# Router weights held in TensorE and tokens moved; routing of both token tiles in shared VectorE operations, experts chosen from the logits

## The reference

```
def moe_swiglu(h, router, w_gate, w_up, w_down):      # h: 256 x 1024, router: 1024 x 8
    probs = softmax(h @ router)
    vals, idx = top_k(probs, 2)
    gates = one_hot(idx) weighted with vals / sum(vals)   # 256 x 8
    for e in range(8):                                    # w_gate, w_up: 1024 x 2048, w_down: 2048 x 1024
        out += gates[:, e] * ((silu(h @ w_gate[e]) * (h @ w_up[e])) @ w_down[e])
```

## Time and profile before

| | before |
|---|---|
| median of 3 runs | 1415.55 us |
| lowest, highest | 1414.0, 1416.23 us |
| the profiled execution: its time | 1413.8 us |
| its span, first to last instruction | 1411.8 us |
| mean granted TensorE clock | 0.957 of 2.4 GHz |
| PE busy | 1323.1 us (94%) |
| DVE busy | 1049.4 us (74%) |
| ACT busy | 864.3 us (61%) |
| POOL busy | 38.8 us (3%) |
| mean DMA rate | 226 GB/s |

### The profile page before, as it was taken

How to read it: one execution, slowest core, us unless ns; L and a number is a source line. 1 busy time by engine, 2 the same in 40 slices (tenths; PEclk the granted TensorE clock), 3 DMA queues, 4 the chain that set the end, 5 groups by cost and what they waited for, 6 DMA issues and landing times.

```text
span 1411.8 us, 18829 instructions
## 1 busy us (share of the span) xinstructions
PE 1323.1 (94%) x6088; PEld 1080.8 (77%) x6088; DVE 1049.4 (74%) x1488; ACT 864.3 (61%) x1274; POOL 38.8 (3%) x54
## 2 busy tenths in 40 slices
PE   7999999997687899999999999999997985999998
PEld 5878888886566788888888888888886753888887
DVE  4576555565755799999999999999995846555554
ACT  4655444456533587878787887878784544454443
POOL 0000000000300000000000000000000211000000
PEclk9999999998887999999999999999998977999999
DMA  9645545554013397979898999889894400355540
GB/s 356 217 143 207 179 179 191 195 178 150 1 60 120 147 383 296 383 299 377 316 367 330 340 342 337 338 338 371 325 375 134 179 30 1 119 182 195 188 150 30
DMA packets 46121, 319.30 MB, mean 226 GB/s; under 512 B 5152, under 2 KB 6304, under 8 KB 7808
## 3 DMA queue, kind: packets, MB, share of 16 engines
q1 hardware_dynamic: 44288, 316.39, 59.7%
q10 hardware_dynamic: 1680, 2.10, 0.5%
q0 software_dynamic: 112, 0.26, 0.1%
HBM read 316.64 MB, written 2.10 MB: 226 GB/s over the span
## 4 chain that ended last, share of the span: by engine, by line
PE 84%; DVE 9%; issue 3%; ACT 3%; DMA 1%; DVEq 0%; POOL 0%; SPq 0%; ACTq 0%; POOLq 0%
PE bank L350 24%; PE bank L352 24%; PE bank L351 24%; PE bank L641 2%; PE bank L414 2%; DVE wl L1223 2%; DVE x L1637 1%; PE bank L744 1%; PE bank L386 1%; DMA fixed<-fixed_dram 1%; PE bank L660 1%; PE bank L661 1%; PE bank L765 1%; PE bank L581 0%; PE bank L803 0%
## 5 line engine op out<-in xcount | busy, mean ns | idle before, releaser
L1223 DVE TENSOR_TENSOR wl<-raw,wh 128x1024 fp32r<-128x1024 f32 x598 | 714.8, 1221 | 208.5 <-ACT wh L828 197.7
L828 ACT ACTIVATE wh<-raw 128x1024 fp32r<-128x1024 f32 x598 | 631.4, 1061 | 327.3 <-PE bank L352 320.6
L350 PE MATMUL bank<-wh,xth 128*128 128x512 f32 (+2 forms) x1170 | 464.1, 397 | 15.0 <-DVE wl L1223 4.7
L352 PE MATMUL bank<-wh,xtl 128*128 128x512 f32 (+2 forms) x1170 | 455.4, 389 | 0.0
L351 PE MATMUL bank<-wl,xth 128*128 128x512 f32 (+2 forms) x1170 | 455.1, 389 | 0.0
L350 PEld LDWEIGHTS bank<-wh,xth 128*128 128x128 f32 x1170 | 221.8, 190 | 61.2 <-issue 7.7
L352 PEld LDWEIGHTS bank<-wh,xtl 128*128 128x128 f32 x1170 | 221.4, 189 | 46.2
L351 PEld LDWEIGHTS bank<-wl,xth 128*128 128x128 f32 x1170 | 222.2, 190 | 42.3
L350 PE MATMUL bank<-wh,hth 128*128 128x512 f32 x456 | 178.5, 391 | 0.0
L352 PE MATMUL bank<-wh,htl 128*128 128x512 f32 x456 | 177.9, 390 | 0.0
L351 PE MATMUL bank<-wl,hth 128*128 128x512 f32 x456 | 177.4, 389 | 0.0
(11 more groups left out here) (281 smaller groups left out, 853.5 us busy)
## 6 DMA issues: line engine op xcount, KB each, us to landing
raw<-weights_dram SPq DMA_DIRECT2D x299, 1024.0 KB, 4.9
x<-x_dram SPq DMA_DIRECT2D x1, 1024.0 KB, 7.7
bias_scratch<-act ACTq DMA_DIRECT2D x1, 1024.0 KB, 15.7
wide<-bias_scratch ACTq DMA_DIRECT2D x8, 128.0 KB, 2.6
out_dram<-x SPq DMA_DIRECT2D x4, 256.0 KB, 2.1
fixed<-fixed_dram SPq DMA_DIRECT2D x1, 596.0 KB, 8.8
rows<-rows_dram POOLq DMA_DIRECT2D x1, 256.0 KB, 6.1
cols<-cols_dram SPq DMA_DIRECT2D x1, 73.0 KB, 8.5
```

Of the source, the lines that this page charges most:

```text
L350: mm(o, lh, wh[:, wi, sl], start=start, stop=False)
L352: return mm(o, ll, wh[:, wi, sl], start=False, stop=stop)
L828: A(wh[:, c % SPLIT, :], raw[:, (c // 2) % RAW, (c % 2) * UNIT:(c % 2 + 1) * UNIT], ACT.Copy).then_inc(hi_done, 1)
L1223: V.tensor_tensor(wl[:, c % SPLIT, :], raw[:, (c // 2) % RAW, (c % 2) * UNIT:(c % 2 + 1) * UNIT], f32(wh[:, c % SPLIT, :]), ALU.subtract). ...
```

## The change

It does five things.

1. The router's high and low weights become one tile `rw` of 16 columns for each block of 128 and are the stationary operand; `xth` and `xtl` (256 tokens) move past it. That gives 16 matmuls into 16 rows of logits parts by 256 tokens, half of them ahead of the second `turn_half`. ACT copies the 16x256 result to SBUF, and two small fp32 matmuls with a constant (`fold`, two stacked 8x8 identities) add the two parts and turn them back to tokens by experts. Low times low, left out before, is now in the sum.
2. DVE works on both token tiles in shared operations, and picks the experts from the logits; softmax comes no more.
3. The gates are made later, from the difference of the two largest logits with one small exponential on ACT; this DVE work stands between `sel` and `gathered`.
4. The five matmuls for places and counts become two for places ahead of the gather and two for counts (`bank[3]`) behind it; the copy to `queue` moves behind `gathered(0)`. Five fills of constants move ahead of the output projection, and ACT's part of `xn` moves behind the copy of the logits.
5. PE waits for the gathered blocks two at a time, ahead of each gate and up unit, in all 8 experts.

On PE:

```diff
             out_proj(U_WO, "ffn1")
+            def route(ks):
+                for k in ks:
+                    for x_part in (xth, xtl):
+                        last = mm(bank[0][0:2 * NE, 0:TOK], rw[:, k, :], x_part[:, k, :], start=(k == 0 and x_part is xth),
+                                  stop=(k == KD - 1 and x_part is xtl))
+                return last
+            pe.wait_ge(sem("rt_l"), 1)
+            pe.wait_ge(sem("norm_l"), KD * nth("ffn1") + 4)
+            route(range(0, 4))
             turn_half("ffn1", 1, 6)
-            pe.wait_ge(sem("norm_l"), KD * (nth("ffn1") + 1))
-            pe.wait_ge(sem("rt_l"), 1)
+            pe.wait_ge(sem("norm_l"), KD * nth("ffn1") + KD)
+            route(range(4, 8)).then_inc(sem("rt_L"), 1)
+            fold = fixed[0:2 * NE, FIXED["fold"]:FIXED["fold"] + NE]
+            pe.wait_ge(sem("rt_Lc"), 1)
             for t in range(NT):
-                for k in range(KD):
-                    h, l = xt(k, t)
-                    o = bank[t][:, 0:NE]
-                    mm(o, h, rth[:, k * NE:(k + 1) * NE], start=(k == 0), stop=False)
-                    mm(o, h, rtl[:, k * NE:(k + 1) * NE], start=False, stop=False)
-                    last = mm(o, l, rth[:, k * NE:(k + 1) * NE], start=False, stop=(k == KD - 1))
-                last.then_inc(sem("rt_S"), 1)
+                last = mm(bank[1][:, t * NE:(t + 1) * NE], ebuf[0:2 * NE, 0, t * P:(t + 1) * P], fold, start=True, stop=True)
+            last.then_inc(sem("rt_S"), 1)
-            pe.wait_ge(sem("chosen"), NT)
-            mm(bank[0][:, 0:NE], before, chosen[:, 0, 0:NE], start=True, stop=True)
-            mm(bank[0][:, 16:16 + NE], before, chosen[:, 1, 0:NE], start=True, stop=False)
-            mm(bank[0][:, 16:16 + NE], ones, chosen[:, 0, 0:NE], start=False, stop=True)
-            mm(bank[0][:, 32:32 + NE], ones, chosen[:, 0, 0:NE], start=True, stop=False)
-            mm(bank[0][:, 32:32 + NE], ones, chosen[:, 1, 0:NE], start=False, stop=True).then_inc(sem("places"), 1)
+            pe.wait_ge(sem("chosen"), 1)
+            mm(bank[2][:, 0:2 * NE].rearrange("p (t n) -> p t n", t=NT), before, chosen[:, :, 0:NE], start=True, stop=False)
+            mm(bank[2][:, NE:2 * NE], ones, chosen[:, 0, 0:NE], start=False, stop=True).then_inc(sem("places"), 1)
...
             gather("moe", sel, 1, CAP)
+            for t in range(NT):
+                last = mm(bank[3][:, 0:NE], ones, chosen[:, t, 0:NE], start=(t == 0), stop=(t == NT - 1))
+            last.then_inc(sem("counts"), 1)
             with pe.Fori(0, NE) as e:
-                pe.wait_ge(sem("moe_gl"), e * KD + KD)
                 ffn("ff", U_MOE, FFE // FG, 2, 3, FG, 2, e * 4, e, nt=1, done=DONE_FF1,
-                    early=lambda: scatter_and_turn(e), late=lambda: gather_next(e))
+                    early=lambda: scatter_and_turn(e), late=lambda: gather_next(e),
+                    rows_ready=lambda u: pe.wait_ge(sem("moe_gl"), e * KD + 2 * u + 2))
```

On ACT (the exponential before, L1064, goes), where `out_proj` has ended with the second half's `xth`:

```diff
             rs_ready("ffn1")
+            sc.wait_ge(sem("rt_L"), 1)
+            A(ebuf[0:2 * NE, 0, 0:TOK], bank[0][0:2 * NE, 0:TOK], ACT.Copy).then_inc(sem("rt_Lc"), 1)
             A(xn[:, 1, :], x[:, 1, :], ACT.Copy, scale=nrs[:, 1:2]).then_inc(sem("norm_xn"), 1)
+            sc.wait_ge(sem("rt_d"), 1)
+            A(small[:, 64:66], small[:, 62:64], ACT.Exp).then_inc(sem("rt_e"), 1)
```

On DVE; the loop over t that goes is L1551 to L1575, 17 operations for each tile:

```diff
+            link(V.memset(ones, 1.0))
+            link(V.memset(gates[:, :, :], 0.0))
+            link(V.memset(f32(selt[:, :]), 0.0))
+            link(V.memset(chosen[:, :, :], 0.0))
+            link(V.memset(place[:, :, :], 0.0))
             out_proj(U_WO, "ffn1")
             dv.wait_ge(sem("norm_rs"), nth("ffn1") + 1)
             V.tensor_scalar(xn[:, 0, :], x[:, 0, :], nrs[:, 0:1], None, ALU.mult)
-            link(V.memset(ones, 1.0))
-            link(V.memset(gates[:, :, :], 0.0))
-            link(V.memset(f32(selt[:, :]), 0.0))
...
+            dv.wait_ge(sem("rt_S"), 1)
+            link(V.tensor_tensor(lg, bank[1][:, 0:2 * NE].rearrange("p (t n) -> p t n", t=NT),
+                                 nrs[:, 0:NT, None].to_broadcast((P, NT, NE)), ALU.mult))
+            for t in range(NT):
+                r = V.max(top[:, t, :], lg[:, t, :])
+                link(r) if t else mark(r)
+            for t in range(NT):
+                r = V.max_index(topi[:, t, :], top[:, t, :], lg[:, t, :])
+                link(r) if t else mark(r)
+            link(V.tensor_copy(fi, topi[:, :, :]))
+            mark(V.tensor_tensor(first, io, fi[:, :, 0:1].to_broadcast((P, NT, NE)), ALU.is_equal))
+            link(V.tensor_tensor(second, io, fi[:, :, 1:2].to_broadcast((P, NT, NE)), ALU.is_equal))
+            V.tensor_tensor(chosen[:, :, 0:NE], first, second, ALU.add).then_inc(sem("chosen"), 1)
+            V.tensor_tensor(small[:, 62:64], top[:, :, 1], top[:, :, 0], ALU.subtract).then_inc(sem("rt_d"), 1)
             dv.wait_ge(sem("places"), 1)
-            link(V.tensor_copy(place[:, :, 0:NE], bank[0][:, 0:32].rearrange("p (t n) -> p t n", t=NT)[:, :, 0:NE]))
-            link(V.tensor_copy(queue[:, 0:NE], bank[0][:, 32:32 + NE]))
+            link(V.tensor_copy(place[:, :, 0:NE], bank[2][:, 0:2 * NE].rearrange("p (t n) -> p t n", t=NT)))
...
             ins.then_inc(sem("moe_sel"), 1)
+            dv.wait_ge(sem("rt_e"), 1)
+            link(V.tensor_scalar(small[:, 66:68], small[:, 64:66], 1.0, None, ALU.add))
+            link(V.reciprocal(small[:, 68:70], small[:, 66:68]))
+            link(V.tensor_tensor(small[:, 70:72], small[:, 64:66], small[:, 68:70], ALU.mult))
+            mark(V.tensor_tensor(first, first, small[:, 68:70, None].to_broadcast((P, NT, NE)), ALU.mult))
+            link(V.tensor_tensor(second, second, small[:, 70:72, None].to_broadcast((P, NT, NE)), ALU.mult))
+            link(V.tensor_tensor(gates[:, :, 1:NE + 1], first, second, ALU.add))
             gathered(0)
+            dv.wait_ge(sem("counts"), 1)
+            link(V.tensor_copy(queue[:, 0:NE], bank[3][:, 0:NE]))
```

More of the change, by code:

```diff
@@ L98 @@
 for _name, _n in (("ident", 128), ("mask", 384), ("ctab", 128), ("stab", 128), ("freq", 32), ("iota", 8),
-                  ("before", 128), ("slots", 128), ("every", 128)):
+                  ("before", 128), ("slots", 128), ("every", 128), ("fold", 8)):
     FIXED[_name] = _at
@@ L157, in build @@
         selt = sb("selt", [P, TOK], F32R)
-        rth = sb("rth", [P, KD * NE], F32R)
-        rtl = sb("rtl", [P, KD * NE], F32R)
+        rw = sb("rw", [P, KD, 2 * NE], F32R)
         small = sb("small", [P, 128])
@@ L465, in ffn @@
                 else:
-                    up(c0, i0)
+                    up(c0, i0, rows_ready)
                     early()
@@ L1057, in _ @@
                     A(xth[:, h, :], bank[4 + h % 2][:, 0:256], ACT.Copy).then_inc(sem("head_oh"), 1)
-            A(rth[:, :], cols[:, COLS["router"]:COLS["router"] + 64], ACT.Copy).then_inc(sem("rt_h"), 1)
+            A(rw[:, :, 0:NE], cols[:, COLS["router"]:COLS["router"] + 64].rearrange("p (k n) -> p k n", k=KD), ACT.Copy)\
+                .then_inc(sem("rt_h"), 1)
             out_proj(U_WO, "ffn1")
             rs_ready("ffn1")
+            sc.wait_ge(sem("rt_L"), 1)
+            A(ebuf[0:2 * NE, 0, 0:TOK], bank[0][0:2 * NE, 0:TOK], ACT.Copy).then_inc(sem("rt_Lc"), 1)
             A(xn[:, 1, :], x[:, 1, :], ACT.Copy, scale=nrs[:, 1:2]).then_inc(sem("norm_xn"), 1)
[L1062 to L1065, removed]
+            sc.wait_ge(sem("rt_d"), 1)
+            A(small[:, 64:66], small[:, 62:64], ACT.Exp).then_inc(sem("rt_e"), 1)
             def gathered(lot):
@@ L1541, in _ @@
             dv.wait_ge(sem("rt_h"), 1)
-            V.tensor_tensor(rtl[:, :], cols[:, COLS["router"]:COLS["router"] + 64], f32(rth[:, :]), ALU.subtract).then_inc(sem("rt_l"), 1)
+            V.tensor_tensor(rw[:, :, NE:2 * NE], cols[:, COLS["router"]:COLS["router"] + 64].rearrange("p (k n) -> p k n", k=KD),
+                            f32(rw[:, :, 0:NE]), ALU.subtract).then_inc(sem("rt_l"), 1)
+            link(V.memset(ones, 1.0))
[3 more added lines that the diff above has]
+            link(V.memset(place[:, :, :], 0.0))
             out_proj(U_WO, "ffn1")
@@ L1545, in _ @@
             V.tensor_scalar(xn[:, 0, :], x[:, 0, :], nrs[:, 0:1], None, ALU.mult)
-            link(V.memset(ones, 1.0))
-            link(V.memset(gates[:, :, :], 0.0))
-            link(V.memset(f32(selt[:, :]), 0.0))
-            for t in range(NT):
[L1551 to L1576, removed]
@@ L1577, in _ @@
-            link(V.memset(place[:, :, :], 0.0))
+            lg, top, fi, first, second = (small[:, 16 * n:16 * (n + 1)].rearrange("p (t n) -> p t n", t=NT) for n in (0, 1, 2, 5, 6))
+            io = fixed[:, None, FIXED["iota"]:FIXED["iota"] + 8].to_broadcast((P, NT, NE))
+            dv.wait_ge(sem("rt_S"), 1)
+            link(V.tensor_tensor(lg, bank[1][:, 0:2 * NE].rearrange("p (t n) -> p t n", t=NT),
```

(8 more changed lines are left out.)

## The result

The changed kernel took 1397.47 us in the median of 4 runs (1395.94 to 1398.22), the kernel before 1415.52 (1414.0 to 1416.23): ratio 0.9873, 95% interval 0.9855 to 0.989, 18.05 us less. Forecast were 1405.3 us, 10.2 us less, and 1402.0 to 1408.4 as range. The direction was right; the time lies 4.5 us outside the range.

What follows compares the result with a forecast made beforehand. PE was taken to bound the whole kernel (84% of the chain). The gather 10.75 us earlier, less 0.35 for its clock and 0.21 for the queue copy, gave 10.2 off 1415.55: 1405.3 us, range 1402.0 to 1408.4.

Steps and rivals of the forecast that it cites:

- first router half: Eight router matmuls in PE's pause after the output projection: cost 0, or 0.96 us without that cover.
- second router half: Eight router matmuls once `xtl` is ready, at half the clock with spacing 0.24: 2.1 us, bounds 1.2 and 3.6.
- routing on DVE: Shared DVE operations for both token tiles, after the fold: 1.9 us against 4.42, bounds 1.5 and 2.3.
- gather, later clock: First gather: the clock's rise comes 0.7 us later after its start, costing 0.35 us; bounds 1.9 either way.
- queue copy behind `gathered`: Copy to `queue` now on DVE's chain into the first expert: 0.21 us back.
- waits by twos: PE's waits for gathered blocks: gain 0, PE's first-turn pause about 2.4 us; rival that they pay: 1403.5 us, chance 0.05.
- net at both turns: From router to the first expert's turns: 10.75 less 0.35 less 0.21, 10.2 us gained.
- That bound: Lower bound for the router's second eight matmuls, at the full clock: 1.2 us.
- The gates are hidden as said: Six DVE operations between select and `gathered`, covered by the wait for the gather: cost 0, without cover 1.2 us.
- the rival's price: Pause at expert 0's first turn drops TensorE's clock: 1.6 us lost, 3 if longer; 1406.9 us, chance 0.25.
- the step to the total: What comes ahead of the expert loop moves the kernel's end one for one: 10.2 us off the median.
- the sign: Prediction is wrong if the span after expert 0's second turn differs in length from before.

Runs made afterwards that it cites:

- before_fillA: The kernel before with 29 matmuls that nothing reads, ahead of and in the last layer's first attention: 1411.1 us.
- after_serial: The changed kernel with gates, count matmuls and queue copy put back ahead of the gather: 1400.1 us in 2 runs.
- the three delayed ones: The changed kernel with 7, 14 or 21 linked fills on DVE ahead of select, a pure delay: 1404.77, 1403.52 and 1402.33 us.
- 7 fills: The changed kernel with 7 linked fills of 8 columns on DVE ahead of select: 1404.77 us.
- fillABM: Both kernels with 169 unread matmuls at the experts' end and around both last-layer attentions, none in the routing: before 1404.25 us, changed 1393.85.
- fillA: Both kernels with 29 unread matmuls ahead of and in the last layer's first attention: before 1411.1 us, changed 1400.26.
- before_router: The kernel before with the new router alone, DVE's routing still tile by tile: 1412.22 us, ratio 0.9982.
- after_again: The changed kernel, unchanged, run in a second session: 1402.37 us, ratio 0.9912.
- after_third: The changed kernel, unchanged, run in a third session: 1401.85 us, ratio 0.9912.

## Why the prediction was right and wrong

**Right: the stretch.** 11.1 us up to the loop's end against 10.2. By its terms, measured against forecast, in us:

| term | forecast | measured |
|---|---|---|
| first router half | 0 | 0 |
| second router half | 2.1 | 1.18 |
| copy of the logits | 0.44 | 0.43 |
| fold | 1.14 | 1.06 |
| routing on DVE | 1.9 | 1.62 |
| places | 1.14 | 1.13 |
| copy and select | 0.96 | 0.96 |
| sum, against 18.43 before | 7.68 | 6.38 |
| gather, later clock | 0.35 back | 0.83 back |
| queue copy behind `gathered` | 0.21 back | 0.41 back |
| waits by twos | 0 | not measured at the full clock |
| net at both turns | 10.2 | 10.8 |

That the net came out within 0.6 us is partly luck. The gather starts 12.05 us earlier and not 10.75, and two terms behind it, 0.7 us dearer together than forecast, take half of that back.

The biggest miss is the second router half. I took the low clock, since it had fallen by then in the kernel before; here it was still up (0.12 us spacing, 442.26 and 442.38). That bound was in the text, at 1.2. It was no chance of this one execution. With the first half in the pause ahead, the clock fell 6.6 to 7.1 us behind the start of the last projection matmul in all eleven traces without filling in the routing. In the kernel before it fell 3.6 us behind it in three traces, but 6.6 in the fourth (before_fillA), so even there the low clock wasn't sure. My doubled spacing of 0.24 was too dear as well: in before_fillA 14 matmuls with 256 columns moving, 128 stationary, took 3.00 us at the low clock, 0.21 each, which agrees with the estimate of 0.213 from the Trainium skill (TensorE: Matmul & The Clock Gate, section on the back-to-back issue gap). With 16 stationary columns no run shows the low spacing. On DVE an operation over 16 elements costs what one over 8 does (0.17 to 0.18 us), and the unlinked one of each pair costs 0.07 to 0.1. The gather's clock came back 5.5 us after its start and not 4.4. The last 0.3 us, between the second turn and the loop's end (10.8 to 11.1), lie in the loop; I did not follow them, and they are less than the 1.2 by which that stretch differs between traces of the changed kernel.

The gates are hidden as said: their last operation starts at 449.29, and DVE then waits 4.21 us for the gather's first half. Counts and queue copy would put the gather off by 1.05 us if they stood ahead of it (after_serial, expected 1.06), but with the clock back sooner the first turn by 0.12 only. What the waits by twos gained PE it gave back as forecast, in a pause of 3.01 us for `hbuf` (forecast 2.4). The pause kept the clock at 1.00 in the changed kernel's three traces and in five of its filled and changed variants, but it fell behind it in the three delayed ones, where the two turns lie 10.1 us apart and not 8.8: 1.3 us, the rival's price (1.6). The trace with 7 fills, pause and what follows:

```profile
465.00:469.00 4.00, 0.79 (x6) 0.52 (x5) 3.96 (x6) 0.38 (x1) 0.00 (x0) 1.00 0.26 59
469.00:473.00 4.00, 4.00 (x12) 3.10 (x11) 4.00 (x8) 1.44 (x2) 0.00 (x0) 0.57 0.95 367
```

Twelve matmuls in 4 us at 0.57. That rival is real: it came in 3 of 11 traces, its chance was put at 0.25. But it came in none of the three traces of the changed kernel itself, and in all three with a delay; whether the delay has a part in it isn't shown.

**Wrong: the step to the total.** The step that failed is the one that carries the net of the stretch to the end, 10.2 us off the median of before: it took what lies outside for equally long in both kernels, and gave it nothing in the range. It differs. The prediction had named the sign, a different length behind the second turn of expert 0: from there to the end of the span are 925.5 us before, and 919.0, 922.5 and 926.8 in the three traces of the changed kernel. The attention of the last layer took 28.9 to 37.0 us in the traces, with the same code but for the filling; the start of the routing lay between 436.7 and 439.6. In the kernel before, PE worked in that attention for most of 36 us and the clock stayed low for long; I read the clock there only for its pauses and not for what it would do when everything comes 11 us sooner. With the clock mostly held there in both, the change is worth 10.4 and 10.8 us (fillABM, fillA), which the forecast had. The result's 18 are these and a good clock: 6.8 of the 17.9 us between the profiles lie outside the stretch, and the mean clock is 0.968 in all four runs, of which one has a trace. The kernel before varies too: 1409.5 to 1419.4 in the 16 runs beside before_router, 1413.2 to 1417.0 in the 24 beside the delays and after_again.

The Trainium skill offers a cause (TensorE: Matmul & The Clock Gate, section on what's actually happening): the window in which the clock's monitor watches the engine is "free-running — it doesn't reset when your kernel starts". The runs agree that the course varies with nothing changed (the attention's 31.5, 33.1 and 37.0 us); that this is the reason no run here shows.

**Open.** Unfilled, the changed kernel gains 12 to 13 us in the later sessions and not 10.6, so it may meet a better clock a little more often than the kernel before; 14 runs against a spread of 9 us don't settle it. Nor is it shown why the first session's four runs were all fast, or whether the chip has a part in it: after_again ran on another chip than after_third, and that of the first session isn't on record.

## What to carry to other kernels

Put the rows of a change together as a chain and the stretch can be forecast, here to a microsecond with some luck among the terms; the total can't, where other stages run PE in bursts, as this attention does, since their clock can be another in each execution. Compare such kernels by landmarks in the trace, or in several sessions, or with PE's pauses filled in both (look in the trace whether the filling lies in the pause or behind it), and give the range the spread of those stages. Where an engine's second batch hides its partner's first, a faster engine alone brings that first batch onto the chain: the router gave 3.6 us of its 7.8 until DVE's work was shared too.

## What the runs showed of the hardware

- The clock stayed low under a PE that was busy nearly all the time. In the last layer's first attention, in the kernel before, a mean clock of 0.72 stood beside 31.06 busy us of 36.2, and four score matmuls of 64 rows took 2.07 us in it at the low clock; in the old router ten busy us of 8-column matmuls stayed at 0.50 (the earlier trace rows shows seven of them).
- 29 matmuls that nothing reads, about 3.5 us of PE time at the full clock, took 3.3 us off the kernel before, though 14 of them ran behind a pause and not in it; 216 took 11 to 12 off the changed one (1401.85 and 1402.37 to 1390.71, across sessions).
- A pause of 3.0 us of PE in dense work kept the clock in eight traces and was followed by a fall in three.
- A stationary operand of 16 columns with 256 moving keeps the spacing of 0.12 us that 128 columns have at the full clock; at the low clock 128 columns with 256 moving have 0.21 (before_fillA).
